# Attention stage of an encoder layer: the row-maximum products taken on 64 rows, two heads in one slot out of two, the turned score products four slots later

## Chip, cores and metric

The kernel runs on one core of one Trainium2 chip. The metric is the device time of one execution in microseconds. The kernel before has a median of 1143.6 us over three runs (1142.76 to 1144.29).

## What is computed

One encoder layer over two sequences of 512 tokens (model width 1024), written in float32. The part that matters here is the attention of group A: eight query heads and two key/value heads of width 64, softmax over all 512 keys.

```python
def global_gqa_attention(q, k, v):
    ...
    def one_block(q_blk):
        sc = jnp.einsum('bkgqd,bksd->bkgqs', q_blk, k).astype(jnp.float32) * scale
        p = jax.nn.softmax(sc, axis=-1).astype(v.dtype)
        return jnp.einsum('bkgqs,bksd->bkgqd', p, v)
```

Group B is a neighbourhood attention with eight heads of its own. Both groups' outputs are normalised, joined and multiplied by an output matrix; a wide MLP with squared ReLU and a last normalisation follow. A softmax doesn't change when the same number is subtracted from all scores of a row, so the maximum that guards the exponential need not be exact.

## The kernel before, in words

Float32 operands of the projections are split into a high and a low part (type fp32r), and the products are made of these parts. The projections before attention, the attention stage, the output projection and the MLP follow one another on TensorE.

**The attention stage** is a hand-written loop over slots. Each engine runs through the same slots in its own order, and semaphores keep them in step. There are 64 units of group A (two sequences, eight heads, four blocks of 128 queries or keys) and 64 units of group B. NSLOT is 75.

In slot s, TensorE issues in this order (lines 1304 to 1321):
- `score_turned` (lines 1222 and 1223), for the unit of six slots ago (LAG_S = 6): the scores with keys along the partitions. The first product has q's high and low part on 128 rows; the second has the keys' low part, and also q's shift (minus the row's maximum) by way of rows that hold ones.
- `score_b` (line 1237): two products of 256 columns for group B, into the one bank B_BANK. It waits until the unit before it was read by VectorE.
- `score_max` (line 1206): one product of 128x128 by 512 columns, q's high and low rows against the high part of the keys doubled over both halves. It serves only to find each row's maximum.
- `turn_b` (line 1249): two transposes of group B's probabilities.
- `values_a` (line 1264): probabilities by values for the unit of ten slots ago (LAG_VA = 10); four products, each of which the trace shows as two.
- `values_b` (line 1286), for three slots ago; two products, each shown as two.
- every eighth slot or so `turn_prep` (line 1183), the transposes that bring a pair of heads' q (or the second sequence's k) into place, and from slot 54 on, every second slot, `turn_y` (line 1301).

VectorE goes through slot s in this order (lines 2341 to 2362): `head_out` of group A and of group B, once in four slots each (lines 2328 and 2331); `row_max` of the slot before (line 2279), and after the fourth of a head `row_shift` (line 2291, two instructions), which writes the maxima as a diagonal into q_hd; `bias_max` of group B (line 2306); `prep_low` (line 2234) two and three slots after a turn_prep; later `y_low` (line 2338). It is strictly in this order.

ScalarE makes the exponentials (lines 1742 and 1749), copies turned probabilities (line 1757) and makes the high parts (line 1687). GpSimd stages group B's operands. SyncE's queue copies stacks for group B, k's high part to the other half (k_landed) and each head's q to q_hd (`copy_q`, lines 733 to 742). `copy_slot` gives the slot of each copy, from LAG_S and PREPS.

The scores of group A use PSUM banks 0 to 2 in rotation. The list A_EVENTS gives the order of the products that take a bank, and `wait_a_bank` (line 1163) lets a product wait for the reader of the third product before it: VectorE's row_max for a maximum, ScalarE's exponential for turned scores.

Once its last slot is done, TensorE begins the output projection (lines 1056 to 1058).

Of the kernel before, what the change touches and what calls it, by code (L numbers as in the profile page):

```python
# [24 lines left out]
AX_X = mybir.AxisListType.X  # L25

P = 128
# [5 lines left out]
TPB = NT // NB  # L33
DT = D // P
HD = 64
AH, KVH, BH = 8, 2, 8
# [36 lines left out]
NA, NBS = NB * AH * TPB, NB * BH * TPB  # L73
A_ORDER = [0, 4, 1, 5, 2, 6, 3, 7]
A_HEADS = [(b, h) for b in range(NB) for h in A_ORDER]
# [5 lines left out]


A0 = 0
LAG_S, LAG_VA = 6, 10
LAG_PB, LAG_VB = 2, 3
NSLOT = NA + A0 + LAG_VA + 1
A_BANKS, OB_BANK, PT_BANK, PREP_BANK, OA_BANK, B_BANK = (0, 1, 2), 3, 4, 5, 6, 7
# [2 lines left out]


PREPS = [(None, ("K", 0)), (None, ("Q", 0)), (4, ("Q", 1)), (8, ("Q", 2)), (16, ("Q", 3)), (20, ("K", 1)),
         (24, ("Q", 4)), (32, ("Q", 5)), (40, ("Q", 6)), (48, ("Q", 7))]
Y_SQUARE, Y_RMS, Y_RECIP, Y_TURN, W_SPLIT = 43, 51, 52, 54, 69
EARLY_PREPS = 2
EARLY_TURN, EARLY_HIGH, EARLY_LOW = 2, 4, 5
PREP_NO = {p: n for n, (_, p) in enumerate(PREPS)}
# [8 lines left out]


def smax_at(s):
    return s - A0 if 0 <= s - A0 < NA else None


def st_at(s):
    return s - A0 - LAG_S if 0 <= s - A0 - LAG_S < NA else None


def va_at(s):
    return s - A0 - LAG_VA if 0 <= s - A0 - LAG_VA < NA else None


def y_turn_at(s):  # L120
    return (s - Y_TURN) // 2 if 0 <= s - Y_TURN < 4 * TPB and (s - Y_TURN) % 2 == 0 else None


def b_at(s, lag=0):
    return s - lag if 0 <= s - lag < NBS else None


A_EVENTS = []
for _s in range(NSLOT):
    if st_at(_s) is not None:  # L130
        A_EVENTS.append(("st", st_at(_s)))
    if smax_at(_s) is not None:
        A_EVENTS.append(("smax", smax_at(_s)))
A_EVENT_NO = {ev: n for n, ev in enumerate(A_EVENTS)}


# [187 lines left out]
def encoder_program(nc, xs_in, w_in, bias_tab, w_gains, norm_mlp_gain, final_gain, qk_gains, w_out, w_up, w_down,  # L324
                    rope_c, mask_c, ident_c, ys_out):
    with ExitStack() as ctx:
        def sb(name, shape, dt=F32, where=ctx):
            return where.enter_context(nc.sbuf_tensor(name, shape, dt))

        def sem(name):  # L330
            return ctx.enter_context(nc.semaphore(name))
# [65 lines left out]
        negmax = sb("negmax", [P, 2, NA], F32, space)  # L397
# [46 lines left out]
        q_hl = sb("q_hl", [P, PAIR_SLOTS, 2, SEQ], F32R, space)  # L444
# [9 lines left out]
        k_hh, k_lo1 = (k_hh_0, k_hh_1), (k_lo1_0, k_lo1_1)  # L454
# [8 lines left out]
        prep_lo = sem("prep_lo")  # L463
        k_landed = [sem(f"k_landed{b}") for b in range(NB)]
# [44 lines left out]
        smax_done = sem("smax_done")  # L509
        max_ready = sem("max_ready")  # L510
# [33 lines left out]
        def over(ap, axis, n):  # L544

            shape = list(ap.shape)
            return ap.unsqueeze(axis).to_broadcast(shape[:axis] + [n] + shape[axis:])
# [434 lines left out]
        def piece_gain(n):  # L982

            if BLOCKS[n // DT].weight == "w_up":
                return None
            return w_gain[:, {"w_in": 0, "w_out": 1}[BLOCKS[n // DT].weight], n % DT:n % DT + 1]
# [35 lines left out]
        def head_rows(h):  # L1022

            return (slice(0, HD), slice(HD, P)) if h < AH // 2 else (slice(HD, P), slice(0, HD))

        def q_slot(u):

            head = u // TPB
            return (head // 2) % PAIR_SLOTS, head % 2
# [11 lines left out]
        def a_bank(ev):  # L1041
            return ps[A_BANKS[A_EVENT_NO[ev] % len(A_BANKS)]]
# [10 lines left out]
        def _(pe):  # L1053
# [109 lines left out]
            def wait_a_bank(ev):  # L1163

                n = A_EVENT_NO[ev] - len(A_BANKS)
                if n >= 0:
                    what, u = A_EVENTS[n]
                    pe.wait_ge(max_ready if what == "smax" else pA_ready, u + 1)
                else:

                    bank = n + len(A_BANKS)
                    pe.wait_ge(dve_evac if bank % 2 else act_evac, ACT0 - 2 + bank // 2 + 1)
# [22 lines left out]

            run_block(6, after_fm(12), early_turns)

            def score_max(u):
                (b, h), q = A_HEADS[u // TPB], u % TPB
                slot, side = q_slot(u)  # L1200
                if q == 0:

                    pe.wait_ge(prep_lo, 1 + max(PREP_NO["Q", u // TPB // 2], PREP_NO["K", b]))
                    pe.wait_ge(k_landed[b], 32)
                wait_a_bank(("smax", u))
                nc.tensor.matmul(a_bank(("smax", u))[:, :], q_hl[:, slot, side, q * P:(q + 1) * P],  # L1206
                                 k_hh[b][:, h // (AH // KVH), :], start=True, stop=True).then_inc(smax_done, 1)

            def score_turned(u):
                (b, h), k = A_HEADS[u // TPB], u % TPB  # L1210
                slot, side = q_slot(u)
                kv = h // (AH // KVH)
                keys = slice(k * P, (k + 1) * P)
                if k == 0:

                    pe.wait_ge(hd_landed[u // TPB % HD_SLOTS], 16 * (u // TPB // HD_SLOTS + 1))
                    pe.wait_ge(shift_ready, u // TPB + 1)
                    if u == 0:
                        pe.wait_ge(ones_ready, 1)
                wait_a_bank(("st", u))  # L1220
                out = a_bank(("st", u))
                nc.tensor.matmul(out[:, :], k_hh[b][:, kv, keys], q_hl[:, slot, side, :], start=True, stop=False)  # L1222
                nc.tensor.matmul(out[:, :], k_lo1[b][:, kv, keys], q_hd[:, (u // TPB) % HD_SLOTS, :], start=False,  # L1223
                                 stop=True).then_inc(st_done, 1)
# [618 lines left out]
        def _(dve):  # L1843
# [429 lines left out]
            run_blocks(0, N_PJ, pj_end)  # L2273


            def row_max(u):

                dve.wait_ge(smax_done, u + 1)
                nc.vector.reduce_max(negmax[:, 0, u:u + 1], a_bank(("smax", u))[:, :], AX_X,
                                     negate=True).then_inc(max_ready, 1)  # L2280

            def row_shift(head):

                (b, h) = A_HEADS[head]
                _, free = head_rows(h)
                u0 = head * TPB
                dve.wait_ge(max_ready, u0 + TPB)
                for half in range(2):
                    rows = slice(half * HD, (half + 1) * HD)
                    dst = q_hd[free, head % HD_SLOTS, :].rearrange("p (q c) -> p q c", c=P)  # L2290
                    ins = nc.vector.tensor_tensor(dst[:, :, half * HD:(half + 1) * HD],
                                                  over(ident[rows, rows], 1, TPB),
                                                  over(negmax[rows, 0, u0:u0 + TPB], 2, HD), ALU.mult)
                ins.then_inc(shift_ready, 1)

            def bias_max(n):

                (b, h), q = B_HEADS[n // TPB], n % TPB
                dve.wait_ge(sB_done, n + 1)
                if n >= SB_SLOTS:  # L2300

                    dve.wait_ge(pB_ready, n - SB_SLOTS + 1)
                if n == 0:

                    dve.wait_ge(rope_done, NT)
                nc.vector.tensor_tensor_reduce(
                    sB[:, n % SB_SLOTS, :], ps[B_BANK][:, 0:KW], biasm[:, B_VARIANT[q], h, :],
                    scale=-1.0, scalar=BIG, op0=ALU.add, op1=ALU.min,
                    accum_out=negmax[:, 1, n:n + 1]).then_inc(maxB_ready, 1)
# [31 lines left out]
            for s in range(NSLOT + 1):  # L2341
                if s and va_at(s - 1) is not None and va_at(s - 1) % TPB == TPB - 1:
                    head_out("A", va_at(s - 1) // TPB)
                if b_at(s, LAG_VB + 1) is not None and b_at(s, LAG_VB + 1) % TPB == TPB - 1:
                    head_out("B", b_at(s, LAG_VB + 1) // TPB)
                if s and smax_at(s - 1) is not None:
                    row_max(smax_at(s - 1))
                    if smax_at(s - 1) % TPB == TPB - 1:
                        row_shift(smax_at(s - 1) // TPB)
                if b_at(s) is not None:  # L2350
                    bias_max(b_at(s))
                for n, (at, _) in enumerate(PREPS):
                    if n >= EARLY_PREPS and s in (at + 2, at + 3):
                        prep_low(n, s - at - 2)
                if s == Y_RECIP:
                    dve.wait_ge(yrms_ready, 1)
                    nc.vector.reciprocal(rstd[:, 1, 0:TPB, :], rms[:, 1, 0:TPB, :]).then_inc(yrstd_ready, 1)
                if y_turn_at(s - 2) is not None:
                    y_low(y_turn_at(s - 2))
                if W_SPLIT + 1 <= s < W_SPLIT + 1 + W_SLOTS:  # L2360
                    n = PIECE_OUT + s - W_SPLIT - 1
                    dve_split(dve, n, n % W_SLOTS, PC, piece_gain(n))
# [226 lines left out]
```

## Time and profile before

| What | Value |
|---|---|
| Median of three runs | 1143.6 us |
| Lowest and highest | 1142.76 and 1144.29 us |
| Span of the profiled execution, first to last instruction | 1143.1 us |
| Mean granted TensorE clock | 0.995 |
| Attention stage, from its first score product to the output projection's first product | 222.68 to 391.83 us |

The profiled execution has no device time of its own beside its span; the span is 0.5 us under the median of the runs. An engine is called busy when an instruction is under way. A matmul's record lasts longer than the distance at which matmuls follow each other, since they are pipelined: what one costs in a stream is the distance between starts. "PEld" is the load of the stationary operand, which can run beside a matmul.

### The profile page before, as it was taken

The numbers are of one execution on the slowest core, as the hardware profiler recorded it, in microseconds if no ns is written. First come the engines' busy times: TensorE is split into PE (matmuls) and PEld (weight loads), VectorE is DVE, ScalarE is ACT, GpSimd is POOL, SyncE is SP. The second block draws the span as 40 slices with busy tenths as digits, with TensorE's granted clock in tenths as the row PEclk, the third lists the DMA queues.
The fourth block names the chain that finished last, engine by engine and source line by source line (L and its number), as shares of the span: only waits on it lengthen the run. The fifth ranks groups of instructions, "written<-read, shape, count | busy, mean of one in ns | idle before, by whom it ended". The sixth has DMA issues, their size and how long they took to land.

```text
span 1143.1 us, 15377 instructions
## 1 busy us (share of the span) xinstructions
PE 1119.6 (98%) x5528; PEld 929.8 (81%) x5528; DVE 772.5 (68%) x1357; ACT 535.6 (47%) x1018; POOL 184.1 (16%) x194
## 2 busy tenths in 40 slices
PE   6999999999999999999999999999999999999995
PEld 5898888789999988888888788888888888888874
DVE  4625414477666556464977998949759669589498
ACT  5521213366676645255334445255264353452555
POOL 2430496121214000200100101001001001010021
PEclk9999999999999999999999999999999999999998
DMA  9522112475445343521210210221112112201204
GB/s 248 129 73 58 47 46 78 113 166 113 85 95 124 108 138 93 161 83 51 75 37 1 74 56 19 74 74 38 56 56 75 37 37 75 71 16 62 74 19 147
DMA packets 54235, 90.97 MB, mean 80 GB/s; under 512 B 5904, under 2 KB 23312, under 8 KB 54160
## 3 DMA queue, kind: packets, MB, share of 16 engines
q1 hardware_dynamic: 54160, 89.99, 28.7%
q8 instruction: 44, 0.72, 0.3%
q14 instruction: 31, 0.25, 0.1%
HBM read 68.97 MB, written 4.19 MB: 64 GB/s over the span
## 4 chain that ended last, share of the span: by engine, by line
PE 93%; DVE 4%; ACT 1%; issue 1%; DMA 1%; SPq 0%; DVEq 0%; ACTq 0%
PE ps L1056 26%; PE ps L1058 26%; PE ps L1057 26%; PE ps L1264 5%; PE ps L1286 2%; PE ps L956 2%; PE ps L1222 1%; DVE xr L2031 1%; PE ps L1237 1%; PE ps L1223 1%; PE ps L1206 1%; PE ps L1249 1%; DVE w_lo L1876 1%; DVE uv_lo L1897 1%; DMA pj<-x_prompt 1%
## 5 line engine op out<-in xcount | busy, mean ns | idle before, releaser
L1056 PE MATMUL ps<-w_hi,uv_hi 128*128 128x512 f32 x448 | 177.6, 396 | 2.3 <-DVE xr L2031 2.1
L1058 PE MATMUL ps<-w_hi,uv_lo 128*128 128x512 f32 x448 | 177.5, 396 | 0.0
L1057 PE MATMUL ps<-w_lo,uv_hi 128*128 128x512 f32 x448 | 177.4, 396 | 0.0
L1056 PE MATMUL ps<-hT,w_hi 128*128 128x512 f32 x448 | 177.1, 395 | 0.0
L1058 PE MATMUL ps<-hT,w_lo 128*128 128x512 f32 x448 | 176.8, 395 | 0.0
L1057 PE MATMUL ps<-hT,w_hi 128*128 128x512 f32 x448 | 176.8, 395 | 0.0
L1006 DVE SCALAR_TENSOR_TENSOR w_lo<-w_raw,w_gain,w_hi 128x512 fp32r<-128x512 f32 (+1 forms) x88 | 69.9, 799 | 140.5 <-ACT w_hi L997 139.7
L2031 DVE TENSOR_TENSOR xr<-ps,xr 128x512 f32<-128x512 f32 x224 | 140.6, 679 | 7.6 <-PE ps L1058 7.1
L997 ACT ACTIVATE w_hi<-w_raw,w_gain 128x512 fp32r<-128x512 f32 (+1 forms) x88 | 61.4, 703 | 171.8 <-PE ps L1058 167.4
L1056 PE MATMUL ps<-w_hi,hT 128*128 128x512 f32 (+1 forms) x320 | 120.7, 377 | 0.0
L1058 PE MATMUL ps<-w_hi,hT 128*128 128x512 f32 (+1 forms) x320 | 119.3, 373 | 0.0
L1057 PE MATMUL ps<-w_lo,hT 128*128 128x512 f32 (+1 forms) x320 | 119.2, 373 | 0.0
L1056 PEld LDWEIGHTS ps<-w_hi,uv_hi 128*128 128x128 f32 x448 | 84.7, 189 | 23.8 <-issue 3.5
L2524 POOL TENSOR_TENSOR sqf<-sqf 128x512 f32<-128x512 f32 x16 | 20.4, 1298 | 503.6 <-DVE w_lo L1876 503.6
L1058 PEld LDWEIGHTS ps<-w_hi,uv_lo 128*128 128x128 f32 x448 | 84.7, 189 | 20.0
L1057 PEld LDWEIGHTS ps<-w_lo,uv_hi 128*128 128x128 f32 x448 | 84.7, 189 | 19.6
L1058 PEld LDWEIGHTS ps<-hT,w_lo 128*128 128x128 f32 x448 | 84.2, 188 | 20.0
L1056 PEld LDWEIGHTS ps<-hT,w_hi 128*128 128x128 f32 x448 | 84.3, 188 | 19.8
L1057 PEld LDWEIGHTS ps<-hT,w_hi 128*128 128x128 f32 x448 | 84.3, 188 | 19.8
L1897 DVE TENSOR_TENSOR uv_lo<-sqf,uv_hi 128x512 fp32r<-128x512 f32 x112 | 76.1, 720 | 14.7 <-ACT uv_hi L1574 13.9
L1574 ACT CAST uv_hi<-sqf 128x512 fp32r<-128x512 f32 x112 | 64.7, 616 | 22.0 <-DVE sqf L2019 20.1
L1482 ACT CAST w_hi<-turn 128x512 fp32r<-128x512 f32 x64 | 36.5, 616 | 75.5 <-PE ps L1058 75.5
(159 smaller groups left out, 2001.1 us busy)
## 6 DMA issues: line engine op xcount, KB each, us to landing
w_raw<-w_in SPq DMA_DIRECT2D x48, 256.0 KB, 2.7
stk<-stg SPq DMA_DIRECT2D x32, 256.0 KB, 3.7
w_raw<-w_out SPq DMA_DIRECT2D x32, 256.0 KB, 2.6
raw<-w_down SPq DMA_DIRECT2D x32, 256.0 KB, 2.9
turn<-w_down SPq DMA_DIRECT2D x32, 256.0 KB, 2.9
w_raw<-w_up SPq DMA_DIRECT2D x24, 256.0 KB, 2.8
turn<-w_up SPq DMA_DIRECT2D x24, 256.0 KB, 2.9
raw<-w_up SPq DMA_DIRECT2D x24, 256.0 KB, 2.9
```

Source lines behind the costliest of these rows:

```text
L956: last = nc.tensor.transpose(norm_bank(m, t, j)[:, d * P:(d + 1) * P], xn[:, t % 2, (4 * j + d) * P:(4 * j + d + 1) * P], ident[:, :])
L997: ins = nc.scalar.mul(w_hi[:, slot, 0:width], src, g)
L1006: ins = nc.vector.scalar_tensor_tensor(w_lo[:, slot, 0:width], src, g, hi, ALU.mult, ALU.subtract)
L1056: nc.tensor.matmul(out, a_hi, b_hi, start=first, stop=False, skip_group_check=onto)
L1057: nc.tensor.matmul(out, a_hi, b_lo, start=False, stop=False, skip_group_check=onto)
L1058: return nc.tensor.matmul(out, a_lo, b_hi, start=False, stop=last, skip_group_check=onto)
L1264: mm = nc.tensor.matmul(ps[a_out_bank(u // TPB)][:, q * VW:(q + 1) * VW], turn_slot(u - q + k)[:, q * P:(q + 1) * P], pj[:, b * TPB + k, c ...
L1286: mm = nc.tensor.matmul(ps[OB_BANK][:, q * VW:(q + 1) * VW], turnB[:, n % PTB_SLOTS, k * P:(k + 1) * P], v, start=(k == 0), stop=(k == nk ...
L1482: nc.scalar.copy(w_hi[:, n % W_SLOTS, :], weight(c, False, v, kt)).then_inc(hi_split, 1)
L1574: nc.scalar.copy(uv_hi[:, u_slot(c, name), kt, :], u_source(name, kt)).then_inc(uv_hi_ready, 1)
L1897: nc.vector.tensor_tensor(uv_lo[:, u_slot(c, name), kt, :], u_source(name, kt), uv_hi[:, u_slot(c, name), kt, :].bitcast(F32), ALU.subtrac ...
L2031: nc.vector.tensor_tensor(dst, ps[v % 2 * 4 + t][:, :], dst, ALU.add).then_inc(c_added, 1)
```

## The change

The maximum products are made from q's high part alone, on the 64 rows where it lies, against the same 64 rows of the keys' high part. Both heads of a pair lie in different halves of the partitions; their two products are issued one after the other, in even slots only, into two banks. Units are numbered anew (`max_unit`): number n is head n % 2 of its pair. LAG_S and LAG_VA go from 6 and 10 to 10 and 14, NSLOT from 75 to 79. The turns of later q pairs move by three slots, the work on y and the first splits of the output matrix by four. VectorE takes the first maximum of a pair ahead of bias_max and the second behind it, in the odd slot that follows; both heads' row_shift fall into that slot when the pair's last block is reached. The wait for k's copy moves from the maximum products to the turned ones.

```diff
-LAG_S, LAG_VA = 6, 10
+LAG_S, LAG_VA = 10, 14
...
-         (24, ("Q", 4)), (32, ("Q", 5)), (40, ("Q", 6)), (48, ("Q", 7))]
-Y_SQUARE, Y_RMS, Y_RECIP, Y_TURN, W_SPLIT = 43, 51, 52, 54, 69
+         (27, ("Q", 4)), (35, ("Q", 5)), (43, ("Q", 6)), (51, ("Q", 7))]
+Y_SQUARE, Y_RMS, Y_RECIP, Y_TURN, W_SPLIT = 47, 55, 56, 58, 73
...
 def smax_at(s):
-    return s - A0 if 0 <= s - A0 < NA else None
+    return s // 2 if s % 2 == 0 and 0 <= s < NA else None
+
+def max_unit(n):
+    return (2 * (n // 2 // TPB) + n % 2) * TPB + n // 2 % TPB
+
+def maxes_before(head):
+    return 2 * (head // 2 * TPB + TPB - 1) + head % 2 + 1
...
-        A_EVENTS.append(("smax", smax_at(_s)))
+        A_EVENTS += [("smax", 2 * smax_at(_s)), ("smax", 2 * smax_at(_s) + 1)]
...
-            def score_max(u):
-                (b, h), q = A_HEADS[u // TPB], u % TPB
-                slot, side = q_slot(u)
+            def score_max(m):
+                pair, q = m // TPB, m % TPB
+                b = A_HEADS[2 * pair][0]
                 if q == 0:
-                    pe.wait_ge(prep_lo, 1 + max(PREP_NO["Q", u // TPB // 2], PREP_NO["K", b]))
-                    pe.wait_ge(k_landed[b], 32)
-                wait_a_bank(("smax", u))
-                nc.tensor.matmul(a_bank(("smax", u))[:, :], q_hl[:, slot, side, q * P:(q + 1) * P],
-                                 k_hh[b][:, h // (AH // KVH), :], start=True, stop=True).then_inc(smax_done, 1)
+                    pe.wait_ge(prep_lo, 1 + max(PREP_NO["Q", pair], PREP_NO["K", b]))
+                wait_a_bank(("smax", 2 * m))
+                wait_a_bank(("smax", 2 * m + 1))
+                for n in (2 * m, 2 * m + 1):
+                    slot, side = q_slot(max_unit(n))
+                    rows = slice(side * HD, (side + 1) * HD)
+                    nc.tensor.matmul(a_bank(("smax", n))[:, :], q_hl[rows, slot, side, q * P:(q + 1) * P],
+                                     k_hh[b][rows, side, :], start=True, stop=True).then_inc(smax_done, 1)
...
                 if k == 0:
+                    pe.wait_ge(k_landed[b], 32)
...
-                if s and smax_at(s - 1) is not None:
-                    row_max(smax_at(s - 1))
-                    if smax_at(s - 1) % TPB == TPB - 1:
-                        row_shift(smax_at(s - 1) // TPB)
+                    row_max(2 * smax_at(s - 1))
                 if b_at(s) is not None:
                     bias_max(b_at(s))
+                if s and smax_at(s - 1) is not None:
+                    row_max(2 * smax_at(s - 1) + 1)
```

`row_max(n)` now reads the bank of number n, writes the column of its unit, and calls `row_shift` itself behind the fourth block of a head.

## Rows read from the trace of the kernel before

**Rows 1.** The page: busy time by engine, and the chain that ended last.
```profile
PE 1119.6 (98%) x5528; PEld 929.8 (81%) x5528; DVE 772.5 (68%) x1357; ACT 535.6 (47%) x1018; POOL 184.1 (16%) x194
...
PE 93%; DVE 4%; ACT 1%; issue 1%; DMA 1%; SPq 0%; DVEq 0%; ACTq 0%
```
**Rows 2.** Windows: slots 0-5, 6-9, 10-63, 64-74 of the attention stage.
```profile
core 0: us, PE busy (x) PEld busy (x) DVE busy (x) ACT busy (x) POOL busy (x), PEclk, DMA share, GB/s
222.68:230.29 7.61, 6.42 (x43) 5.03 (x42) 7.30 (x21) 4.20 (x11) 2.73 (x3) 1.00 0.61 143
230.29:238.03 7.74, 7.58 (x50) 6.21 (x50) 6.95 (x19) 6.38 (x15) 0.92 (x2) 1.00 0.98 211
238.03:377.01 138.98, 138.98 (x1072) 130.04 (x1072) 96.64 (x264) 92.44 (x201) 33.99 (x31) 1.00 0.49 107
377.01:391.83 14.82, 14.82 (x123) 14.04 (x122) 6.98 (x15) 8.21 (x16) 0.00 (x0) 1.00 0.21 69
```
**Rows 3.** Timeline of TensorE over one slot: start, length, engine, line, operation.
```profile
301.96 0.47 PE L1222 MATMUL ps<-q_hl,k_hh 128*128 128x512 f32 x1
302.27 0.39 PE L1223 MATMUL ps<-q_hd,k_lo 128*128 128x512 f32 x1
302.50 0.39 PE L1237 MATMUL ps<-stk 128*128 128x256 f32 x2
302.73 0.39 PE L1206 MATMUL ps<-k_hh,q_hl 128*128 128x512 f32 x1
302.96 0.38 PE L1249 MATMUL ps<-ident,probB 128*128 128x128 f32 x2
303.18 1.00 PE L1264 MATMUL ps<-pj,turnA 128*128 128x65 f32 x8
304.02 0.61 PE L1286 MATMUL ps<-pj,turnB 128*128 128x65 f32 x4
304.44 0.48 PE L1222 MATMUL ps<-q_hl,k_hh 128*128 128x512 f32 x1
```
**Rows 4.** Line 1206 in the whole trace: count and lengths in ns (min/median/max).
```profile
L1206 PE MATMUL ps<-k_hh,q_hl x64: 389/395/503, 222.9 to 375.3; 128*128 128x512 f32 x64
```
**Rows 5.** Groups of VectorE in the attention stage.
```profile
L2279 DVE TENSOR_REDUCE negmax<-ps 128x1 f32<-128x512 f32 x64 | 43.7, 684 | 0.2
L2306 DVE CUSTOM_DVE_ANT_0 sB<-ps,biasm 128x256 f32<-128x256 f32 x64 | 27.0, 422 | 17.2 <-PE ps L1237 16.9
L2291 DVE TENSOR_TENSOR q_hd<-ident,negmax 64x256 fp32r<-64x256 f32 x32 | 15.3, 479 | 0.8
L2331 DVE TENSOR_TENSOR pj<-ps,pinv 128x256 f32<-128x256 f32 x31 | 13.2, 425 | 1.1
L2234 DVE SCALAR_TENSOR_TENSOR q_hl<-ps,q_hl 64x512 fp32r<-64x512 f32 x14 | 9.6, 689 | 0.4
```
**Rows 6.** Timeline of VectorE in the first two slots.
```profile
223.60 0.42 DVE L2306 CUSTOM_DVE_ANT_0 sB<-ps,biasm 128x256 f32<-128x256 f32 x1
...
223.95 0.69 DVE L2279 TENSOR_REDUCE negmax<-ps 128x1 f32<-128x512 f32 x1
224.63 0.42 DVE L2306 CUSTOM_DVE_ANT_0 sB<-ps,biasm 128x256 f32<-128x256 f32 x1
```
**Rows 7.** Waits of TensorE's matmuls in the stage: total us, times, longest.
```profile
PE ps L1237 <- DVE negmax L2306: 1.1, 2, 0.8
```
**Rows 8.** Timeline of VectorE in two steady slots, with a head's output and a shift.
```profile
302.19 0.18 DVE L2328 RECIPROCAL pinv<-ps 128x4 f32<-128x4 f32 x1 [0.59 <-PE ps L1286]
...
302.75 0.68 DVE L2279 TENSOR_REDUCE negmax<-ps 128x1 f32<-128x512 f32 x1
...
304.52 0.69 DVE L2279 TENSOR_REDUCE negmax<-ps 128x1 f32<-128x512 f32 x1
305.25 0.85 DVE L2291 TENSOR_TENSOR q_hd<-ident,negmax 64x256 fp32r<-64x256 f32 x2
306.13 0.42 DVE L2306 CUSTOM_DVE_ANT_0 sB<-ps,biasm 128x256 f32<-128x256 f32 x1
```

More of the change, by code:

```diff
@@ L2273, in _, with row_max @@
             run_blocks(0, N_PJ, pj_end)
-            def row_max(u):
-                dve.wait_ge(smax_done, u + 1)
-                nc.vector.reduce_max(negmax[:, 0, u:u + 1], a_bank(("smax", u))[:, :], AX_X,
+            def row_max(n):
+                u = max_unit(n)
+                dve.wait_ge(smax_done, n + 1)
+                nc.vector.reduce_max(negmax[:, 0, u:u + 1], a_bank(("smax", n))[:, :], AX_X,
                                      negate=True).then_inc(max_ready, 1)
+                if u % TPB == TPB - 1:
+                    row_shift(u // TPB)
             def row_shift(head):
@@ L2286, in row_shift @@
                 u0 = head * TPB
-                dve.wait_ge(max_ready, u0 + TPB)
+                dve.wait_ge(max_ready, maxes_before(head))
                 for half in range(2):
```

## The prediction

> **What bounds the kernel now.** I read the page first: TensorE is busy 98% of the span and holds 93% of the chain that ended last, nothing else holds more than 4% [rows 1]. So a product removed from TensorE's stream is worth its place in that stream, unless another engine becomes the bound. Then the windows over the attention stage [rows 2]. They show three kinds of stretches. In slots 0 to 5 VectorE is busy 7.30 of 7.61 us, and in slots 6 to 9 6.95 of 7.74: VectorE sets the pace, and TensorE's own work is less than its busy time says, since matmul records overlap their neighbours' gaps. In slots 10 to 63 TensorE is busy all the time (138.98 of 138.98 us) and VectorE 70%. In slots 64 to 74 TensorE alone matters. The granted clock is 1.00 in all four.
>
> The timeline of one steady slot gives prices by distance between starts [rows 3]: turned scores 0.31 + 0.23 = 0.54 us, group B's scores 0.23, the maximum product 0.23, transposes 0.22, values A 0.84, values B 0.42; the slot is 2.48 us. The record of line 1206 lasts 0.39 us [rows 4], but its place is 0.23. Eight products of values A take 0.84, so a load of weights with a short matmul costs 0.105. Line 1222, which comes behind short matmuls, takes 0.08 more than line 1223: its load isn't hidden.
>
> **Part 1, the maximum products.** Removed: 64 products at 0.23 to 0.24 in the stream. I use 0.235, 15.0 us in all. In an odd slot group B's second product (256 columns, 0.12) hides the transposes' first load, so the full 0.235 goes. Added: 32 pairs on 64 rows at an unknown price X each; the trace of before has no product on 64 rows. Bounds from the nearest rows: from below 0.24, one product's place, both streaming at once. From above: both stream at once, but the second's load comes after the first began (0.105), and TensorE empties before and after the pair; a record outlasts its place by 0.39 - 0.23 = 0.16, and a load that isn't hidden adds 0.08, so X = 0.235 + 0.105 + 2 x (0.16 + 0.08) = 0.82. One after the other, they would cost 0.47. I take X = 0.235 + 0.105 + 0.08 = 0.42: side by side, the second a load later, and one load laid bare. It is nearest to what lines 1264 and 1222 show of loads in this stream [rows 3].
>
> A page bears on this. Of the Trainium skill, TensorEngine Tiling (Array Packing), Key Properties, says that changing the tiling mode drains TensorE. The page TensorE: Matmul & The Clock Gate, Part 3, has row tiles start some 4 ns apart. The first speaks for X near 0.82, the second for 0.24; no row of the kernel before shows either.
>
> **Part 2, the first ten slots.** VectorE's work in them is the same after the change: one row_max and one bias_max a slot, two heads' shifts, two prep_lows, one head_out. One row_max with one bias_max takes 0.35 + 0.68 = 1.03 us, start to start [rows 6], and they took 15.35 us before, of which VectorE worked 14.25 [rows 2]. Group B's next score waits for bias_max, so TensorE can't run ahead; this is where its waits on line 2306 lie [rows 7]. After the change TensorE has 4 x 0.54 us less turned scores there and ten maximum products as five pairs. None of it shortens the stretch. So the four turned scores, which now run in the tail, cost their whole place: +2.2 us. And only the pairs of slots 10 to 63 count in part 1: 54 x 0.235 = 12.7 removed, 27 X added.
>
> The order gets a little worse too. In slot 7 VectorE does head_out, row_max, shift, bias_max, row_max, shift and prep_low, and the pair of slot 8 waits for that prep_low (prep_lo). Laying these out with the durations of [rows 5, 6, 8] brings slot 10 to 15.8 us behind the first score instead of 15.35: +0.5. In slots 10 to 13 TensorE has about 1.5 us a slot (no values A yet) and VectorE about the same; two turned scores wait there for row_max, some 0.3 each: +0.6. Between 0 and 1.5 for the two together would not surprise me.
>
> **Part 3, the pile in every eighth slot.** When a pair's fourth block is reached (slots 15, 23, ... 55), both shifts fall into one slot of VectorE. Let slot 14 start at 0; with X = 0.42 slot 15 starts at 2.67 and slot 16 at 4.92. VectorE's head_out starts 0.23 after the slot (302.19 against 301.96 [rows 3, 8]): 2.90. Its pieces: head_out 0.56, row_max 0.73 up to the shift, shift 0.88 (305.25 to 306.13) [rows 8], bias_max 0.35, row_max 0.69 [rows 6]. The second row_max ends at 2.90 + 0.56 + 0.73 + 0.88 + 0.35 + 0.69 = 6.11. The pair in slot 16 is due at 4.92 + 0.54 + 0.23 = 5.69, and waits for that row_max, since it takes the bank again (the third product before it). Late by 0.42. Behind it on TensorE stand the transposes and both values products, so it is lost: slots 16, 24, 32, 40, 48 and 56, 6 x 0.42 = 2.5 us. Slots without the double shift have 0.4 us to spare. X doesn't matter here: it moves both sides alike. Bounds: nothing, if VectorE gets to head_out early, and 3.5, if other delays add.
>
> **Part 4, moved at no cost.** NSLOT grows by four, but the work is the same: four turned scores (counted) and four values A sets (4 x 0.84) go from inside to the tail, where TensorE is busy throughout (14.82 of 14.82) and ScalarE 8.21 [rows 2]. An exponential must end within the next slot's 1.4 us; it does so now. Turn_prep moves by three slots and is still finished a slot before its first use; q_hl's three pair slots are free by then. On SyncE's queue copy_q waits for turned scores that come four slots later and its own slot moves along, seven slots ahead of its reader as before; load_stack behind it still has eight. The k_landed wait moves to a later product. If the queue fell behind by over a slot, group B's scores would feel it; I see no reason.
>
> **Sum** on the profiled execution (span 1143.1): -12.7 + 27 x 0.42 (11.3) + 2.2 + 0.5 + 0.6 + 2.5 = +4.4, so 1147.5; the median of the runs lies 0.5 above the span: **1148.0 us**. With both ends of X: 0.24 gives -0.4, 0.82 gives +15.2.
>
> **Rivals.**
> - *Side by side at full value, but VectorE keeps its price* (X 0.24 to 0.34): -0.4 to +2.3, 1143.2 to 1146. For it: two halves of the rows and two banks share nothing. Against: two loads in a row behind a product of only 0.12. Chance 0.25.
> - *Faster*: X = 0.24 and the pile of part 3 doesn't reach TensorE, nor do the small delays of part 2: -12.7 + 6.5 + 2.2 = -4.0, 1139.6. It decides at the pair of slot 16: if VectorE's second row_max ends before 5.5 us, it holds. For it: VectorE is only 70% busy there [rows 2]. Against: its order is fixed, and the sum of part 3. Chance 0.17.
> - *A drain each way*: TensorE empties when it goes to 64 rows and again when it comes back, X 0.6 to 0.82: +9.3 to +15.2, up to 1158.8. For it: such products depend on another division of the array than the neighbours; against: no row. The rule of the tiling page named above would do this. Chance 0.25.
> - *The change doesn't do what it says*: products on half the rows follow one another as any two do, X = 0.47: +5.8, 1149.4. It lies within my own case.
>
> **How the numbers follow.** My own case (X 0.38 to 0.5, with its neighbours) has 0.33, and gives 1146 to 1150.5. About 0.2%, 2.3 us, is what a measurement of this kernel can tell from no change. Faster by more: 0.17, the second rival. Within: the first rival, 0.25. Slower: 0.58, the rest. The range takes in the first rival's lower bound with some error below it and nearly all of the drain: 1141 to 1159; left out is most of the second rival.
>
> **What would show it.** In the profile after: the distance from the first product of line 1206's successor to the transposes behind it is X: 0.24, 0.42, 0.47 or 0.8. Odd slots last 2.25 us. The stage's tenth slot begins 15.5 to 16 us after its first score, with VectorE over 90% busy. In slots 16, 24 and so on the pair starts some 0.4 us late, released by row_max. I am wrong if even slots last as long as before and all pairs start on time (faster), or if the loads in front of and behind each pair stand bare (a drain).

## The result, and the profile after

The changed kernel takes 1159.26 us (median of four runs, 1157.86 to 1164.15) against 1143.65 us before. The ratio is 1.0143, 95% interval 1.0131 to 1.0155: **slower, by 15.6 us**. I had forecast 1148.0 and slower, in a range from 1141 to 1159: the direction was right, the size far too small.

The page of the changed kernel looks as before at first sight:

```profile
PE 1127.6 (98%) x5528; PEld 928.7 (80%) x5528; DVE 773.4 (67%) x1357; ACT 533.4 (46%) x1018; POOL 183.8 (16%) x194
...
PEclk9999999989999999999999999999999999999998
...
PE 93%; DVE 4%; issue 1%; ACT 1%; DMA 1%; SPq 0%; DVEq 0%; ACTq 0%
```

TensorE is busy 98% and holds 93% of the chain, as in [rows 1], although half of its maximum products should have become free. Busy time says nothing here. In the row of the granted clock (PEclk) one digit differs from the kernel before, which has a 9 in all slices but the last: the 8 in the ninth slice of the span. The windows place it, 6.8 us at 0.50, which is 1.2 GHz (columns as in [rows 2]; the stage now runs from 222.46 to 405.40):

```profile
222.46:234.70 12.24, 9.36 (x61) 6.84 (x59) 10.56 (x30) 6.54 (x16) 2.75 (x3) 1.00 0.76 174
234.70:241.50 6.80, 5.31 (x23) 4.61 (x24) 4.29 (x10) 2.35 (x6) 3.67 (x4) 0.50 0.69 154
241.50:249.86 8.36, 8.36 (x54) 6.67 (x53) 6.46 (x18) 6.82 (x15) 0.00 (x0) 1.00 0.95 211
249.86:381.07 131.21, 128.98 (x963) 113.64 (x961) 85.09 (x232) 80.12 (x179) 30.93 (x28) 1.00 0.38 81
...
383.33:405.40 22.07, 21.45 (x170) 19.89 (x170) 10.07 (x23) 11.86 (x22) 0.00 (x0) 1.00 0.40 117
```

**Where the time went.** The attention stage lasts 182.9 us instead of 169.15 (+13.8). I cut it at two points that both traces have: group B's score product of slot 16, and the start of slot 64.

| Part of the stage | Before | After | Difference |
|---|---|---|---|
| first score product to group B's of slot 16 | 30.9 | 33.35 | +2.5 |
| from there to the start of slot 64 | 123.45 | 127.5 | +4.1 |
| slot 64 to the output projection | 14.8 | 22.1 | +7.25 |

The last line is mostly debt: four turned scores and four values A sets (5.5 us), two more turns of y (0.75), two waits of 0.5. It would be harmless if the first part had become 5.5 us shorter, since that work left it. It became longer.

**The pair itself.** TensorE in an even slot (slot 20, whose further transposes at its end are not shown):

```profile
266.06 0.48 PE L1235 MATMUL ps<-q_hl,k_hh 128*128 128x512 f32 x1
266.38 0.39 PE L1236 MATMUL ps<-q_hd,k_lo 128*128 128x512 f32 x1
266.61 0.40 PE L1250 MATMUL ps<-stk 128*128 128x256 f32 x2
266.94 0.50 PE L1218 MATMUL ps<-k_hh,q_hl 64*128 64x512 f32 x2
267.37 0.44 PE L1262 MATMUL ps<-ident,probB 128*128 128x128 f32 x2
267.64 1.00 PE L1277 MATMUL ps<-pj,turnA 128*128 128x65 f32 x8
```

Two products on 64 rows take 0.50 us together from the first's start to the second's end. The line's group says how long one is (ns, min/median/max):

```profile
L1218 PE MATMUL ps<-k_hh,q_hl x64: 463/492/793, 222.8 to 378.7; 64*128 64x512 f32 x64
```

So they run side by side. But what stands around them has changed against [rows 3]: group B's scores (line 1250, once 1237) hold 0.33 instead of 0.23, the pair 0.43, the transposes (line 1262, once 1249) 0.27 instead of 0.22. An even slot without such transposes or a late pair is 2.84 us; without any maximum product it is 2.26, as the odd slots show. The pair costs 0.58, two full products cost 0.47. The weight loads show why. The kernel before, around line 1206:

```profile
261.66 0.40 PE L1206 MATMUL ps<-k_hh,q_hl 128*128 128x512 f32 x1
261.54 0.19 PEld L1206 LDWEIGHTS ps<-k_hh,q_hl 128*128 128x128 f32 x1
261.68 0.36 PEld L1249 LDWEIGHTS ps<-ident,probB 128*128 128x128 f32 x2
```

and after, around the pair:

```profile
266.94 0.19 PEld L1218 LDWEIGHTS ps<-k_hh,q_hl 64*128 64x128 f32 x2
267.36 0.20 PEld L1262 LDWEIGHTS ps<-ident,probB 128*128 128x128 f32 x2 [0.24 <-issue]
```

Before, the transposes' weights began to load 0.14 us after the maximum's, while its product (from 261.66) streamed. Now the load starts 0.42 us after the pair's own, when the pair's record (266.94 to 267.43) is nearly over. In this trace no load runs ahead across the change of the number of rows.

**The piles of shifts.** In every eighth slot the pair is late, as forecast. VectorE and TensorE around slot 32:

```profile
297.06 0.85 DVE L2307 TENSOR_TENSOR q_hd<-ident,negmax 64x256 fp32r<-64x256 f32 x2
297.94 0.43 DVE L2322 CUSTOM_DVE_ANT_0 sB<-ps,biasm 128x256 f32<-128x256 f32 x1
...
298.29 0.69 DVE L2293 TENSOR_REDUCE negmax<-ps 128x1 f32<-128x512 f32 x1
```

```profile
298.13 0.40 PE L1236 MATMUL ps<-q_hd,k_lo 128*128 128x512 f32 x1
298.52 0.47 PE L1250 MATMUL ps<-stk 128*128 128x256 f32 x2
299.08 0.50 PE L1218 MATMUL ps<-k_hh,q_hl 64*128 64x512 f32 x2
```

Group B's product starts 0.39 after line 1236 instead of 0.23 (it waits for bias_max), and the pair 0.56 after that instead of 0.33 (row_max ends at 298.98). Together 0.40 us, at slots 24, 32, 40, 48 and 56.

**Slot 16 is another matter.** There group B's product came 2.11 us after line 1236. The list of waits names VectorE:

```profile
PE ps L1250 <- DVE negmax L2322: 4.2, 4, 1.7
PE ps L1218 <- DVE q_hl L2247: 1.4, 1, 1.4
```

(The second is the pair of slot 8, waiting for prep_low.) VectorE and GpSimd in slot 15:

```profile
251.91 0.68 DVE L2293 TENSOR_REDUCE negmax<-ps 128x1 f32<-128x512 f32 x1
252.24 1.27 POOL L2486 TENSOR_TENSOR stg<-qkb,stg 128x512 fp32r<-128x512 f32 x1
252.62 2.58 DVE L2307 TENSOR_TENSOR q_hd<-ident,negmax 64x256 fp32r<-64x256 f32 x2
253.47 1.46 POOL L2487 TENSOR_TENSOR stg<-qkb,stg 128x512 fp32r<-128x512 f32 x1
255.24 0.42 DVE L2322 CUSTOM_DVE_ANT_0 sB<-ps,biasm 128x256 f32<-128x256 f32 x1
```

A shift that takes 0.85 us elsewhere took 2.58, and bias_max stood behind it. Slot 16 is late by 2.1 us. The kernel before has the same long shift, and nothing of TensorE's waits behind it:

```profile
252.96 2.33 DVE L2291 TENSOR_TENSOR q_hd<-ident,negmax 64x256 fp32r<-64x256 f32 x2
```

### The profile page after: what moved, and what is told of

Its sections match the earlier page's. It is cut to its first block, busy times and chain, and to the rows that moved or that the text cites. A ratio compares the mean times of both kernels' runs of the same rounds, so it can differ in the third digit from the quotient of the medians.

```text
span 1155.8 us, 15408 instructions
## 1 busy us (share of the span) xinstructions
PE 1127.6 (98%) x5528; PEld 928.7 (80%) x5528; DVE 773.4 (67%) x1357; ACT 533.4 (46%) x1018; POOL 183.8 (16%) x194
## 4 chain that ended last, share of the span: by engine, by line
PE 93%; DVE 4%; issue 1%; ACT 1%; DMA 1%; SPq 0%; DVEq 0%; ACTq 0%
PE ps L1064 26%; PE ps L1066 26%; PE ps L1065 26%; PE ps L1277 4%; PE ps L1299 2%; PE ps L964 2%; PE ps L1262 2%; PE ps L1235 1%; PE ps L1250 1%; PE ps L1236 1%; PE ps L1218 1%; DVE xr L2044 1%; DVE w_lo L1889 1%; DVE uv_lo L1910 1%; DMA pj<-x_prompt 1%
```

## The experiments

Theory D: the two products run side by side, and what costs is going to 64 rows and back. Beside it the schedule has costs of its own: the lag, the double shifts, the wait in slot 8 with the low clock, the long shift in slot 15. Rival S: the number of rows costs nothing and the schedule is all of it. Rival R: the two products don't really overlap. All times are medians; the kernel before took 1143.0 to 1143.6 in the same series.

**Full rows in the new schedule (a_full).**

```diff
-                    nc.tensor.matmul(..., q_hl[rows, slot, side, ...], k_hh[b][rows, side, :], ...)
+                    nc.tensor.matmul(..., q_hl[:, slot, side, ...], k_hh[b][:, side, :], ...)
```

> The changed kernel with its whole schedule, but each maximum product on all 128 rows again (with the wait for the copied keys). Theory D (the pair does run side by side, and what costs is going to 64 rows and back, some 0.35 us a pair): the even slots shrink from 2.84 to 2.73 us, because two full products cost 0.47 and the products around them lose their 0.09 and 0.05; over 27 to 32 pairs that is 3 to 4 us less than the changed kernel, so about 1154 to 1156. Rival S (the form costs nothing, the schedule is all of the loss): no difference from the changed kernel, 1158 to 1160.

Measured: 1155.96 us (1.0109, 1.0094 to 1.0124), 3.3 us under the changed kernel. The even slot is 2.71 us, from line 1235 to the next:

```profile
300.97 0.47 PE L1235 MATMUL ps<-q_hl,k_hh 128*128 128x512 f32 x1
...
301.51 0.39 PE L1250 MATMUL ps<-stk 128*128 128x256 f32 x2
301.75 0.62 PE L1218 MATMUL ps<-k_hh,q_hl 128*128 128x512 f32 x2
302.21 0.38 PE L1262 MATMUL ps<-ident,probB 128*128 128x128 f32 x2
...
303.68 0.47 PE L1235 MATMUL ps<-q_hl,k_hh 128*128 128x512 f32 x1
```

Group B's 0.24, two products 0.46, transposes 0.21. As D expected for the slot; S falls. Doing twice the array work is cheaper than halving it here. The 3.3 us of the whole kernel fit D's 3 to 4 partly by luck: in this trace the pairs that wait for VectorE in slots 24 to 56 are late by 0.72 us instead of 0.40, which takes back 1.6 us, and its low clock lasts 3.4 us instead of 6.8, so that slots 0 to 9 are 0.6 shorter. Why the late pairs cost more with full rows stays open. The run full_shift below, without late pairs, is the clean test.

**The pair issued twice (a_twice).** Same operands, same banks, the first two results overwritten.

> The changed kernel with each pair of 64-row products issued twice in a row (same operands, same banks; the first two are overwritten). Theory D: the second pair needs no change of the array's division and streams at one product's price, so the distance from the first product to the transposes grows from 0.43 to 0.65 to 0.70 us. Rival R (the two don't overlap, their equal starts are only how they are recorded): it grows by 0.43 to 0.47, to about 0.9.

Measured (one execution, 1163.1 us): 0.67 from the first of the four to the transposes, 0.24 more than one pair.

```profile
305.89 0.40 PE L1255 MATMUL ps<-stk 128*128 128x256 f32 x2
306.21 0.74 PE L1220 MATMUL ps<-k_hh,q_hl 64*128 64x512 f32 x4
306.88 0.44 PE L1267 MATMUL ps<-ident,probB 128*128 128x128 f32 x2
```

A second pair costs one product's place. So the overlap is real and R falls; 0.58 - 0.235 = 0.35 us is the price of the two changes of form, with one pair between them or two.

**One product on 64 rows in the old schedule (b_half).** Q's high part alone, one head a slot.

```diff
-                nc.tensor.matmul(a_bank(("smax", u))[:, :], q_hl[:, slot, side, q * P:(q + 1) * P],
-                                 k_hh[b][:, h // (AH // KVH), :], ...)
+                rows = slice(side * HD, (side + 1) * HD)
+                nc.tensor.matmul(a_bank(("smax", u))[:, :], q_hl[rows, slot, side, q * P:(q + 1) * P],
+                                 k_hh[b][rows, h // (AH // KVH), :], ...)
```

> The kernel before, its schedule untouched, each slot's maximum product on 64 rows of q's high part alone. Theory D: every slot pays the change to 64 rows and back for one product, 0.3 to 0.35 us in each of about 56 slots that TensorE bounds: 1160 to 1164. Rival S: no change, 1143 to 1144. Between them, 1149 to 1150, if only one load of 0.1 us a slot is laid bare.

Measured: 1162.6 us (1.0167, 1.0150 to 1.0184), +19.4 us: 0.35 us in 55 slots.

```profile
300.46 0.40 PE L1238 MATMUL ps<-stk 128*128 128x256 f32 x2
300.78 0.49 PE L1207 MATMUL ps<-k_hh,q_hl 64*128 64x512 f32 x1
301.21 0.44 PE L1250 MATMUL ps<-ident,probB 128*128 128x128 f32 x2
```

The distances (0.32, 0.43, 0.27) are those of the pair: one product or two, the same. The schedule is untouched, so this is the cleanest proof that the change of form costs what D says.

**The lag alone (b_lag).** The kernel before with LAG_S, LAG_VA = 10, 14 and the times of the q turns and of the work on y moved as in the change.

> The kernel before with nothing but the four slots more of lag (10 and 14, the turns of q and the work on y moved as in the change); one full product in every slot. My account of the changed kernel puts 2.5 us of lateness at slot 16 plus 5.5 us of work moved behind it against the front of the stage, of which the double shift in slot 7, the lower clock after it and the double shift in slot 15 are part. Here no double shift exists. If the lag alone does it (the first ten slots keep their length because of VectorE): 2 to 4 us more than before, 1146 to 1148. If the double shifts and the clock do it: under 2.2 us, 1144 to 1146. If the lag also drops the clock: 1149 or more.

Measured: 1146.6 us (1.0032, 1.0020 to 1.0044), +3.4: the first case. Slots 0 to 9 last 14.89 us with VectorE busy 14.26, and the clock stays at 1.00:

```profile
221.78:236.67 14.89, 12.51 (x84) 9.84 (x82) 14.26 (x39) 8.71 (x21) 3.29 (x4) 1.00 0.79 178
```

That is hardly shorter than the 15.35 us of [rows 2], though four turned scores are gone from there. VectorE sets that length. The tail is 0.5 us longer than the work moved into it. The rest of the changed kernel's 15.6 us isn't the lag.

**The double shifts apart (a_shift).** The first head's shift goes behind the second row_max, the second head's into the next slot.

```diff
-                if u % TPB == TPB - 1:
-                    row_shift(u // TPB)
...
                     row_max(2 * smax_at(s - 1) + 1)
+                    if smax_at(s - 1) % TPB == TPB - 1:
+                        row_shift(2 * (smax_at(s - 1) // TPB))
+                if s > 1 and smax_at(s - 2) is not None and smax_at(s - 2) % TPB == TPB - 1:
+                    row_shift(2 * (smax_at(s - 2) // TPB) + 1)
```

> The changed kernel with the two row_shifts of a pair taken apart and out of the way of the maxima: the first head's behind the second row_max of the odd slot, the second head's one slot later, behind bias_max. If the double shift is what makes every eighth pair late (0.40 us, five times between slots 24 and 56) and bias_max late in slot 15 (1.9 us, where a shift took 2.58 us for its usual 0.85 while GpSimd worked), the lateness goes in all six places and slot 8 begins its pair up to 0.9 us sooner: 3.5 to 5 us less than the changed kernel's 1159.3, so 1154 to 1156. If the lateness has another releaser (turned scores, the stacks' copies), it stays: 1158 to 1160. If VectorE only meets GpSimd elsewhere: 1156 to 1158.

Measured: 1151.9 us (1.0081, 1.0060 to 1.0102), 7.4 less than the changed kernel and more than I had expected. In the trace the five late pairs (2.0 us) and the lateness of slot 16 (2.1) are gone. The other 3.3 us are not shown by it: the profiled execution is the slowest of the four (1156.2, the others 1150.8 to 1152.8), its clock was at 0.50 for 6.8 us from 227.0 on and for 3.4 from 240.6 on, and its slots 0 to 9 last 20.3 us, 1.4 longer than the changed kernel's. That the pair of slot 8 would come sooner isn't borne out there either: it waits 2.22 us for prep_low. The clock fell in this trace before slots 7 and 8, so their waits aren't what brought it down here.

**Waiting for the high part alone (a_high).**

```diff
-                    pe.wait_ge(prep_lo, 1 + max(PREP_NO["Q", pair], PREP_NO["K", b]))
+                    pe.wait_ge(prep_hi, 1 + max(PREP_NO["Q", pair], PREP_NO["K", b]))
```

(and the wait for prep_lo at the head of the turned scores)

> The changed kernel, but the pair waits only for q's high part (all that it reads), and the turned scores wait for the low part. The pair of slot 8 waited for prep_low behind two shifts, until 236.96. It would go some 1.5 us sooner, and with it the transposes and values behind it. If the low clock of slots 8 and 9 follows from that wait, the clock stays high or the low stretch is shorter too: 1.5 to 4 us less, 1155.5 to 1158. If VectorE's own queue (bias_max behind both shifts) sets slot 9 all the same: under 0.7 us less.

Measured: 1154.6 us (1.0110, 1.0085 to 1.0135), 4.6 less. One of the four executions took 1159.4, the others 1153.6 to 1154.9. The low clock stretch of the profiled execution was 3.4 us instead of 6.8, and slots 0 to 9 last 16.7 us instead of 18.9. But slot 16 is late by only 0.4, as in the other piles: here the first head's shift takes 0.86 us, and it is the second head's that meets GpSimd, where nothing of TensorE's stands behind it:

```profile
252.78 1.83 DVE L2308 TENSOR_TENSOR q_hd<-ident,negmax 64x256 fp32r<-64x256 f32 x2
```

VectorE had shifted against GpSimd. 1.7 us of this gain belong to that meeting, not to the wait.

**The pair at the slot's end (a_end).** The call of score_max moves behind values_b.

> The changed kernel with the pair at the end of its slot, behind values B and in front of the next slot's turned scores, rather than between group B's scores and the transposes. Theory D has two prices for a pair, going to 64 rows (0.09) and coming back (the load of the next product can't run ahead). Behind the pair there now stands line 1235, whose load is bare anyway (0.08): so 0.08 of the price is shared, 27 x 0.08 = 2 us less; and the pair comes 1.5 us later than the row_max it waits for, so the 0.40 in every eighth slot goes (2 us less). 1155 to 1156. If going to 64 rows costs as much behind a product of 65 columns as the load of a full product does (0.1 more), the first part is lost: 1157. Rival: the maxima are now 1.5 us later for VectorE, which works in a strict order, and bias_max behind them gets late in the front: 1159 or more.

Measured: 1154.0 us (1.0091, 1.0076 to 1.0106), 5.2 less. My first reason was wrong. Going to 64 rows costs 0.12 there, and coming back

```profile
302.06 0.50 PE L1218 MATMUL ps<-k_hh,q_hl 64*128 64x512 f32 x2
302.49 0.50 PE L1235 MATMUL ps<-q_hl,k_hh 128*128 128x512 f32 x1
302.83 0.39 PE L1236 MATMUL ps<-q_hd,k_lo 128*128 128x512 f32 x1
```

costs the same 0.43, with 0.34 for line 1235 instead of 0.31. The even slot is 2.81 instead of 2.84, but the odd one 2.28 instead of 2.26; the price of the form can't be hidden in the neighbour's bare load. The pairs no longer wait for VectorE (0.40 us, five times), but in slots 30, 38, 46 and 54 values A now start 0.49 us after the transposes instead of 0.21 (VectorE's head_out, which stands behind prep_low there, ends at 290.27):

```profile
289.94 0.38 PE L1262 MATMUL ps<-ident,probB 128*128 128x128 f32 x2
290.43 1.08 PE L1277 MATMUL ps<-pj,turnA 128*128 128x65 f32 x8
```

From group B's product of slot 16 to slot 64 the trace is thus only 0.3 us shorter. The gain lies in front of that (30.7 us instead of 33.35: slot 16 isn't late, as in a_high, and slots 0 to 9 are 1.3 shorter) and in the tail (0.5), with 1.2 us outside the stage.

**Work in the gaps (a_warm).** 19 full products without use in slots 5 to 8.

```diff
+                for _ in range({5: 1, 6: 5, 7: 6}.get(s, 0)):
+                    nc.tensor.matmul(ps[OA_BANK][:, :], k_hh[0][:, 0, 0:P], k_hh[0][:, 0, :], start=True, stop=True)
```

(and seven more in front of the pair of slot 8)

> The changed kernel with 19 products without use (128 rows, 512 columns, into a bank that nothing reads yet) where TensorE would wait in slots 5 to 8. The granted clock fell to half for 6.8 us from 234.7 on, after TensorE had waited long in slots 7 and 8. If the fall follows from these waits, it doesn't come, the products of slots 8 and 9 take half as long, and slot 10 starts 2 to 3 us sooner although work was added: 1156 to 1157.5. If VectorE sets slots 8 to 10 at either clock: no gain, or up to 1 us more, 1159 to 1160.

Measured: 1155.3 us (1.0119, 1.0086 to 1.0152), 4 less with more work. Three of its executions took 1154.4 to 1155.3, the fourth 1163.1; the profile is of the fourth, and there the clock had fallen before the added work began, and again later. The other three had a mean granted clock of 0.995, against 0.988 to 0.993 for the changed kernel. So with the added work three executions of four were faster and had a higher mean clock, but no trace shows where, and these runs don't show that the waits of slots 7 and 8 are what brings the low clock on: the one trace, like a_shift's, shows it beginning earlier. What brings it on stays open.

**GpSimd held back (a_pool).** The fourth staging waits until the double shift of slot 15 is done.

```diff
+                if pair == 3:
+                    pool.wait_ge(shift_ready, 4)
```

> The changed kernel, with GpSimd's fourth staging (it ran from 251.0 to 254.9) held back until the double shift of slot 15 is done. In the changed kernel the first shift there took 2.58 us for its two instructions instead of 0.85, with GpSimd at work beside it. If the two hinder each other: 0.85 again, group B's score product of slot 16 comes 1.5 to 1.9 us sooner, and the kernel is about 1.5 us faster than the changed one, 1157 to 1158 (its own spread, from the low clock, is 6 us, so the trace decides, not the time). If the long shift has another cause: it stays at 2.5 us or so. If the staging is needed sooner: TensorE waits for a stack in slot 24.

Measured: 1154.6 us (1.0098, 1.0081 to 1.0115), and the trace:

```profile
252.08 0.86 DVE L2307 TENSOR_TENSOR q_hd<-ident,negmax 64x256 fp32r<-64x256 f32 x2
252.96 0.43 DVE L2322 CUSTOM_DVE_ANT_0 sB<-ps,biasm 128x256 f32<-128x256 f32 x1
...
254.03 0.85 DVE L2307 TENSOR_TENSOR q_hd<-ident,negmax 64x256 fp32r<-64x256 f32 x2
```

```profile
255.04 0.61 POOL L2486 CAST stg<-qkb 128x512 fp32r<-128x512 f32 x1 [15.22 <-DVE q_hd L2307]
```

The shift is back at 0.86 us, all 32 of its instructions last 416 to 423 ns, and slot 16 is late by the usual 0.40. So the two had hindered each other; this is shown. The kernel gained 4.6 us at the median, of which the trace explains 1.4: 1.7 at slot 16, less 0.3 lost in slots 10 to 13. The front is the same (low clock from 234.5 for 6.8 us), and the rest is within the spread of the executions or unexplained.

**Three mends together (a_all).** a_shift, a_high and a_end in one kernel.

> The changed kernel with three mends together: the shifts taken apart, the pair's wait on q's high part alone, the pair at the slot's end. Each alone gave 7.4, 4.6 and 5.2 us against 1159.3. They share the lateness of every eighth slot (2.0 us) and of slot 15 (up to 1.9), and the wait in slot 8. What no mend touches is the price of the 64 rows (0.57 us a pair against 0.47) and the lag (b_lag: 3.4 us): 1143.6 + 3.4 + 27 x 0.1 = 1149.7. So 1148.5 to 1151. If the gains were separate they would add up to 1142; if there is a cost of the form or the lag that I have not seen, it stays above 1152.

Measured: 1150.8 us (1.0066, 1.0052 to 1.0080), within the expectation, with no low clock in the stage and 14.8 us for slots 0 to 9. The gains weren't separate.

**Full rows with the shifts apart (full_shift).**

> The changed kernel with the shifts taken apart and full products of 128 rows: no price of the 64 rows, no lateness of the shifts, only the schedule of pairs and the lag. Theory D and the sum of its parts: a_shift (1151.9) less 27 to 32 times 0.115 = 1148.2 to 1148.8, and near b_lag's 1146.6 plus what the front's waits still cost. If it comes out at a_shift's own time, the gain of the full products in a_full (3.3 us) belonged to the front, not to each pair.

Measured: 1149.6 us (1.0054, 1.0040 to 1.0068), 2.3 less than a_shift and a little over the expected 1148.8. The trace gives the price of the form by itself: from group B's product of slot 16 to slot 64 it takes 123.1 us, a_shift's 125.8, which is 2.7 us less over 24 pairs, 0.114 each, as the slots of a_full said. Its front still has a low stretch (mean granted clock 0.82 from 222.9 to 240.0 us).

**One slot less lag in the kernel before (b_early).** LAG_S, LAG_VA = 5, 9, the work on y a slot sooner.

> The kernel before with one slot less lag (5 and 9, the work on y a slot sooner): b_lag turned round. Four slots more cost 3.4 us, since VectorE sets the length of the first slots and turned scores taken out of them run in the tail at full price. By the same account one slot less puts one turned score (0.54 us) into the front where TensorE waits: 0.3 to 0.8 us less than before, 1142.5 to 1143.3. If the shift, which now ends about 0.8 us ahead of its reader, comes late in some slots, each adds up to 0.8 us: above 1144.5.

Measured: 1143.57 us against 1142.96 (1.0005, 0.9996 to 1.0014): no difference that can be told. A miss: the gain that I expected from the lag turned round isn't there. The profiled execution has it in part: slots 0 to 9 took in one turned score and one set of values A (1.38 us) and grew by 1.05, so 0.3 was saved. One new wait of 0.5 us, at 345.5, where a maximum product waits for an exponential, takes more than that back. Whether this is the whole reason stays open. No version here beats the kernel before.

## Why the prediction was wrong in size

- **Part 1, X** is the step that failed most. I took 0.42 and measured 0.58 (0.09 + 0.43 + 0.05 around and in the pair): 27 x 0.16 = 4.3 us. The drain that I gave a chance of 0.25 is what happens, just below its forecast span of 0.6 to 0.82: 0.82 assumed that the second product's load came late (it doesn't) and that entering costs 0.24 (0.09). Of the Trainium skill, the rule of TensorEngine Tiling (Array Packing), Key Properties, that changing the mode drains TensorE, agrees with the trace: the next load starts 0.42 us after the pair's instead of 0.14. The rule of the Trainium skill's page TensorE: Matmul & The Clock Gate, Part 3, that row tiles start some 4 ns apart, agrees as well (0.50 us for two, 0.49 for one). I had set them against each other. They don't speak of the same thing: the first is about the edges of the pair, the second about its inside. The likeliest case should have held both, 0.235 + a price for each edge.
- **Part 2, the front**: right that VectorE sets it and that the moved scores cost their full place (b_lag: +3.4). That my terms for the front made 3.3 is partly luck, since 0.5 of them was meant for a double shift that b_lag doesn't have; slots 0 to 9 there are 0.5 shorter than before, and the tail is 0.5 longer than the work moved there. Wrong in slots 0 to 9 of the changed kernel: 18.9 us, not 15.8, and VectorE busy 78% of them, not over 90%. I forecast TensorE waiting there and held the clock at 1.00 all the same, a term set at nothing without a reason. It fell to 0.50 for 6.8 us, and TensorE's own steps then lasted twice as long inside the chain through VectorE: 0.71 for four transposes instead of 0.36. From the pair of slot 8 (236.96) to slot 10 it took 4.4 us; the same steps at full clock elsewhere in the trace add up to 2.4. So about 2.0 of the 3.1 us are the clock, by this estimate. The 0.6 for slots 10 to 13 didn't come: TensorE's own work there is 6.84 us (two slots of 2.84 - 0.84, two of 2.26 - 0.84) and they last 6.95.
- **Part 3, the piles**: right in place and size, 0.40 against the forecast 0.42, five times. At slot 16 it was 2.1, because I priced the shift from a row without GpSimd beside it. 1.7 us missed. The kernel before has the same long shift, hidden by its slack; I had seen only the group's mean [rows 5]. With the longer pairs of a_twice they are still 0.39, as I had said of X, but with full rows (a_full) 0.72.
- **Part 4, nothing lost in the tail**: nearly. I had overlooked that slot 63 has a double shift too, and y_low behind it: 0.5 us, and another 0.5 behind a head_out.
- **The base**: I set the span 0.5 us under the device time, from a span and the times of other executions. In the profiled execution of the changed kernel they lie 2.1 apart (1157.86 and 1155.8). The kernel before was thus profiled in an execution some 1.5 us above its median. Between the profiled executions the loss is 12.7 us, between medians 15.6.

The sum with the measured terms: 4.4 + 4.3 + 3.1 + 1.7 + 1.0 - 0.5 = 14.0, less 1.1 by which the kernel outside the stage was shorter in these two executions, is 12.9, for 12.7 measured.

The direction was given a chance of 0.58, but not by the sum that came true; the range's top of 1159 missed by 0.3 us, since the drain was added to no other mishap. The faster rival fell on its own test: VectorE's second row_max ended after the pair was due.

## What to carry to other kernels

A product on half of the array's rows among full ones cost 0.35 us here for going there and back, with one, two or four of them between; two pairs in a row (0.81 us, a_twice) are cheaper than four full products would be (4 x 0.235 = 0.94, an estimate), one pair (0.58) doesn't beat two (0.47). So group them, or leave the full products alone. When work leaves a stretch, ask which engine sets its length: if it is another one, the work has only been moved to where it costs its full price. And price an instruction from its longest row, not its mean, once it has lost its slack.

## What the runs showed of the hardware that I had not expected

- The two-input VectorE instruction of row_shift took up to 1.40 us (2.58 for a pair, above) instead of 0.42 while GpSimd worked on SBUF, and 0.42 when GpSimd was held back (a_pool). Of the Trainium skill, SBUF — State Buffer, SBUF: two separate sides, says that a VectorE instruction with two SBUF inputs and a GpSimd instruction that reads SBUF lock each other out for a whole instruction. The trace agrees: GpSimd's second instruction took 1.46 us there instead of 1.27, and VectorE's shift ended at 255.20, 0.28 us after it. row_max, with one input from PSUM, kept its 0.68 us where it overlapped the same GpSimd work.
- The granted clock varied between executions of one kernel: 0.993, 0.988, 0.992 and 0.993 for spans of 1155.8, 1162.1, 1157.9 and 1156.3 us. The mean clock lost between the first two, 0.005 of 1160, is 5.8 us, about the 6.3 by which the spans differ. The changed kernel's executions spread over 6.3 us, the kernel before's over 1.4 to 2.8 in the different series. That TensorE's waits at the start of the stage bring the wider spread is not shown.
